# The two borders of a recurrent layer: squares of x while the context is read, sums by column tiles, factors spread ahead of the barrier, context added by GpSimd

## The reference

```python
for layer in range(2):
    shift_l, scale_l, gate_l = split(silu(c) @ ada_w[layer] + ada_b[layer])      # and shift_c, ... for the context
    hl = rmsnorm(xl, norm_pre[layer]) * (1.0 + scale_l) + shift_l
    hc = rmsnorm(xc, norm_pre[layer]) * (1.0 + scale_c) + shift_c
    oc, ol = even_mixer(hc, hl, ...) if layer == 0 else odd_mixer(hc, hl, ...)
    xl = xl + gate_l * rmsnorm(ol, norm_post[layer])
    if layer == 0:
        xc = xc + gate_c * rmsnorm(oc, norm_post[layer])
```

## Time and profile before

| | us |
|---|---|
| three executions | 3513.63, 3516.14, 3526.28 |
| the profiled execution | 3518.56 |
| its span in the profile | 3516.8 |
| PE busy | 3212.9 (91%), 18471 instructions |
| DVE busy | 1626.2 (46%) |
| POOL busy | 1342.6 (38%) |
| ACT busy | 1194.6 (34%) |

### The profile page before, as it was taken

The page is one execution under the profiler, slowest core; times in us unless marked ns, Lnnn a source line. Parts: engine busy times, 40 slices in busy tenths (PEclk is TensorE's granted clock), DMA queues, the critical chain, the costliest instruction groups (busy, mean ns, idle before and its releaser), DMA issues. The chain is left out here.

```text
span 3516.8 us, 49237 instructions
## 1 busy us (share of the span) xinstructions
PE 3212.9 (91%) x18471; PEld 2593.2 (74%) x18471; DVE 1626.2 (46%) x3082; ACT 1194.6 (34%) x2125; POOL 1342.6 (38%) x877
## 2 busy tenths in 40 slices
PE   6999988899998999898999959985988999989996
PEld 5888765688877888676788848873766777768875
DVE  6444386444435653412711044326666645264443
ACT  3222245322223222343322232243444434243342
POOL 3444431344443443333344423242666630133332
PEclk8999989899998999899999979996999999979998
DMA  7555321355544545222433332222222233112211
GB/s 228 187 178 173 112 76 35 120 185 181 171 132 156 175 135 159 76 78 66 141 95 92 98 113 60 70 80 61 49 51 45 62 85 106 36 48 60 60 49 42
DMA packets 636826, 363.03 MB, mean 103 GB/s; under 512 B 109182, under 2 KB 629108, under 8 KB 636144
## 3 DMA queue, kind: packets, MB, share of 16 engines
q1 hardware_dynamic: 632432, 353.48, 34.2%
q10 hardware_dynamic: 3056, 6.29, 0.5%
q0 software_dynamic: 1168, 0.91, 0.1%
HBM read 334.12 MB, written 26.50 MB: 103 GB/s over the span
## 5 line engine op out<-in xcount | busy, mean ns | idle before, releaser
L266 POOL TENSOR_TENSOR w_lo<-w_raw,w_hi 128x1024 fp32r<-128x1024 f32 (+1 forms) x398 | 939.8, 2362 | 1735.7 <-ACT w_hi L258 1735.7
L303 PE MATMUL acc<-h,w_hi 128*128 128x512 f32 x3136 | 978.7, 393 | 6.4 <-POOL w_lo L266 6.4
L258 ACT ACTIVATE w_hi<-w_raw 128x1024 fp32r<-128x1024 f32 (+1 forms) x398 | 414.4, 1042 | 996.5 <-PE acc L303 960.9
L303 PEld LDWEIGHTS acc<-h,w_hi 128*128 128x128 f32 x3136 | 584.0, 188 | 128.5 <-POOL w_lo L266 7.5
L303 PE MATMUL acc<-h,w_lo 128*128 128x512 f32 x1568 | 613.4, 391 | 0.0
L303 PE MATMUL acc<-hid,w_hi 128*128 128x512 f32 x1408 | 437.2, 392 | 0.0
L303 PE MATMUL lat<-h,w_hi 128*128 128x512 f32 x912 | 336.6, 407 | 16.0 <-DVE h L428 13.8
L303 PEld LDWEIGHTS acc<-h,w_lo 128*128 128x128 f32 x1568 | 295.0, 188 | 63.7
L707 DVE SCALAR_TENSOR_TENSOR ada_part<-ada_raw,c_act,ada_part 128x256 f32<-128x256 f32 x672 | 314.9, 488 | 18.6
L303 PEld LDWEIGHTS acc<-hid,w_hi 128*128 128x128 f32 x1408 | 263.6, 188 | 54.3
L303 PE MATMUL acc<-hid,w_lo 128*128 128x512 f32 x704 | 275.1, 391 | 0.0
(11 more groups left out here) (495 smaller groups left out, 5001.3 us busy)
## 6 DMA issues: line engine op xcount, KB each, us to landing
w_raw<-in_ffn_w SPq DMA_DIRECT2D x240, 512.0 KB, 3.9
ada_raw<-in_ada_w SPq DMA_DIRECT2D x88, 1024.0 KB, 5.0
w_raw<-in_od_w_in SPq DMA_DIRECT2D x32, 512.0 KB, 4.0
w_raw<-in_ev_w_in SPq DMA_DIRECT2D x30, 512.0 KB, 3.8
w_raw<-in_ffn_w SPq DMA_DIRECT2D x32, 384.0 KB, 3.4
image<-inverse_wait SPq DMA_DIRECT2D x288, 32.0 KB, 2.1
first_ada<-in_ada_w SPq DMA_DIRECT2D x8, 1024.0 KB, 12.3
w_raw<-in_ab_w_in SPq DMA_DIRECT2D x16, 512.0 KB, 3.9
```

The lines of the kernel that those rows point to most:

```text
L258: act.activation(K.w_hi[:, first % SPLIT, 0:tiles, :], K.raw[:, first % RAW, 0:tiles, :], ACT.Copy).then_inc(K.hi_ready, 1)
L266: pool.tensor_tensor(K.w_lo[:, first % SPLIT, 0:tiles, :], K.raw[:, first % RAW, 0:tiles, :], K.w_hi[:, first % SPLIT, 0:tiles, :].bitcast ...
L303: mm = pe.matmul(out, w[:, slot, k, :], moving(ap, k, tokens), start=first and k == 0 and p == 0, stop=last and k == tiles - 1 and p == le ...
```

## The change

In `even_in_phase` the norm is split in two. ACT squares x alone at once, PE sums the squares of each block directly with `sums_pe` (no adding by DVE), accumulating in a PSUM bank, and the roots and their inverse are made 128 columns wide; the context is transposed in between, and its squares, sums, roots and spread follow, in two tiles of 128 tokens. The splits of the first two weight chunks stand between the steps on ACT. The DVE coefficients (`mu`) come first instead of after the copies.

At the end of `even_out_phase` new functions with `wide_` names take the place of `norm_pe`, `post_dve`, `post_pool` and the `carry_` functions: three column tiles of 256 tokens instead of one-column products, the last block squared before it is copied and summed by PE on its own, the context of all blocks added by POOL, even blocks of x by POOL and odd ones by DVE through PSUM, and the factors for the next layer spread by PE ahead of the barrier into two PSUM banks, `K.spread`, that outlive it. `odd_phase` no longer spreads or waits for a spread.

```diff
@@ norm_dve
-    dve.wait_ge(N.spread, 1)
+    if carried != "spread":
+        dve.wait_ge(N.spread, 1)
@@ new functions
+THIRD = TOK // 3
+def wide_sums_pe(pe, K, out, src, start, stop):
+    for c in range(3):
+        mm = pe.matmul(out[32 * c:32 * c + 32, 0:THIRD], K.ones[:, 0:32], src[:, c * THIRD:(c + 1) * THIRD],
+                       start=start, stop=stop)
+    return mm
+def wide_spread_pe(pe, K):
+    for c in range(3):
+        mm = pe.matmul(K.spread[c // 2][:, (c % 2) * THIRD:(c % 2 + 1) * THIRD],
+                       K.ident[0:96, 32 * c:32 * c + 1].broadcast_to([96, P]), K.roots[0:96, :], start=True, stop=True)
+    return mm
+def wide_roots_act(act, K, sums):
+    return act.activation(K.roots[0:96, :], sums[0:96, 0:THIRD], ACT.Sqrt, scale=1.0 / D, bias=K.eps[0:96])
+def wide_post_pe(pe, K, S, sums):
+    pe.wait_ge(S.post.ssq_added, DB - 1)
+    wide_sums_pe(pe, K, sums, K.ssq, True, False)
+    pe.wait_ge(S.post.sq_ready, DB)
+    wide_sums_pe(pe, K, sums, K.sq[:, (DB - 1) % 2], False, True).then_inc(S.post.ssq_done, 1)
+    pe.wait_ge(S.post.rstd_ready, 1)
+    wide_spread_pe(pe, K).then_inc(S.post.spread, 1)
+def wide_post_dve(dve, K, S, gates, gain, banks):
...
+    for b in range(DB):
+        own, slot = b % 2, (b // 2) % 2
+        if b >= 4:
+            dve.wait_ge((S.x_even, S.x_odd)[own], b // 2 - 1)
+            if own:
+                dve.wait_ge(S.c_odd, b // 2 - 1)
+        lat = banks[slot][:] if own else K.sq[:, slot, LAT]
+        con = (K.ssq, K.var)[slot][:, 0:CTX] if own else K.sq[:, slot, CON]
+        dve.scalar_tensor_tensor(lat, S.y[:, b, LAT], K.fac[:, 0, b:b + 1], K.spread[0][:], ALU.mult, ALU.mult)
+        dve.scalar_tensor_tensor(con, S.y[:, b, CON], K.fac[:, 1, b:b + 1], K.spread[1][:, 0:CTX], ALU.mult,
+                                 ALU.mult).then_inc(S.scaled, 1)
+        if own:
+            dve.wait_ge(S.scaled, b + 1)
+            dve.tensor_tensor(K.x[:, b, :], K.x[:, b, :], lat, ALU.add).then_inc(S.x_odd, 1)
+def wide_post_pool(pool, K, S):
+    for b in range(DB):
+        slot = (b // 2) % 2
+        pool.wait_ge(S.scaled, b + 1)
+        if b % 2:
+            pool.tensor_tensor(K.xc[:, b, :], K.xc[:, b, :], (K.ssq, K.var)[slot][:, 0:CTX], ALU.add).then_inc(S.c_odd, 1)
+        else:
+            pool.tensor_tensor(K.x[:, b, :], K.x[:, b, :], K.sq[:, slot, LAT], ALU.add)
+            pool.tensor_tensor(K.xc[:, b, :], K.xc[:, b, :], K.sq[:, slot, CON], ALU.add).then_inc(S.x_even, 1)
+def wide_carry_pe(pe, K, S, sums):
+    for b in range(DB):
+        pe.wait_ge(S.carry.sq, b + 1)
+        mm = wide_sums_pe(pe, K, sums, S.y[:, b], b == 0, b == DB - 1)
+    mm.then_inc(S.carry.sum, 1)
+    pe.wait_ge(S.carry.root, 1)
+    wide_spread_pe(pe, K)
...
@@ even_in_phase, scalar
-                for n in range(SPLIT):
-                    split_hi(act, K, seg, n, n, 0, DB)
-                act.wait_ge(S.copied, DB)
-                pre_act(act, K, S, pre_mods)
+                act.activation(K.rstd[:, 0:1], K.eps, ACT.Sqrt)
+                for b in range(DB):
+                    if b >= 2:
+                        act.wait_ge(S.x_summed, b - 1)
+                    act.activation(K.sq[:, b % 2, LAT], K.x[:, b, :], ACT.Square).then_inc(S.x_squared, 1)
+                split_hi(act, K, seg, 0, 0, 0, DB)
+                act.wait_ge(S.x_summed, DB)
+                act.activation(root_x, con[0][:, 0:P], ACT.Sqrt, scale=1.0 / D, bias=K.eps).then_inc(S.x_root, 1)
+                split_hi(act, K, seg, 1, 1, 0, DB)
+                for b in range(DB):
+                    act.wait_ge(S.copied, b + 1)
+                    if b >= 2:
+                        act.wait_ge(S.c_summed, b - 1)
+                    act.activation(K.sq[:, b % 2, CON], K.xc[:, b, :], ACT.Square).then_inc(S.c_squared, 1)
+                act.wait_ge(S.c_summed, DB)
+                act.activation(root_c, con[1][0:64, 0:P], ACT.Sqrt, scale=1.0 / D, bias=K.eps[0:64]).then_inc(S.c_root, 1)
+                pre_act(act, K, S, pre_mods, "spread")
@@ even_in_phase, vector
+                dve.wait_ge(S.x_root, 1)
+                dve.reciprocal(root_x, root_x).then_inc(S.x_inv, 1)
+                for b in range(DB):
+                    dve.wait_ge(S.turned, b + 1)
+                    dve.tensor_copy(K.xc[:, b, :], lat[b % 4][:, 0:CTX]).then_inc(S.copied, 1)
+                dve.wait_ge(S.c_root, 1)
+                dve.reciprocal(root_c, root_c).then_inc(S.c_inv, 1)
@@ odd_phase
-        R = [S.psum(f"ret{i}", [P, 512]) for i in range(3)]
+        R = [*K.spread, S.psum("ret2", [P, 512])]
-                norm_pe(pe, S.pre, K, R[0:2], TOK, True)
@@ second_block, ahead of even_out_phase
+        K.spread = [K.psum(ctx, f"factors{i}", [P, 512]) for i in range(2)]
```

More of the change, by code:

```diff
@@ new lines, in wide_post_pool, with wide_carry_act @@
+def wide_post_pool(pool, K, S):
[7 more added lines that the diff above has]
+            pool.tensor_tensor(K.xc[:, b, :], K.xc[:, b, :], K.sq[:, slot, CON], ALU.add).then_inc(S.x_even, 1)
+def wide_carry_act(act, K, S, sums):
+    for b in range(DB):
+        act.wait_ge((S.x_even, S.x_odd)[b % 2], b // 2 + 1)
+        if b % 2:
+            act.wait_ge(S.c_odd, b // 2 + 1)
+        act.activation(S.y[:, b, LAT], K.x[:, b, :], ACT.Square)
+        act.activation(S.y[:, b, CON], K.xc[:, b, :], ACT.Square).then_inc(S.carry.sq, 1)
+    act.wait_ge(S.carry.sum, 1)
+    wide_roots_act(act, K, sums).then_inc(S.carry.std, 1)
@@ L2773, in even_out_phase @@
         unread = S.sb("unread", [P, 1])
+        K.roots = S.sb("norm_roots", [P, THIRD])
         mo = S.sb("m", [P, 2, DB, TOK], F32R)
         S.y = u
-        bank = [S.psum(f"out{i}", [P, 512]) for i in range(8)]
+        bank = [S.psum(f"out{i}", [P, 512]) for i in range(6)] + K.spread
         zc = u[:, ZC_ROW:ZC_ROW + 4, :].rearrange("p b t -> p (b t)")
```

87 lines of the change are left out of this document (68 added, 19 removed).

## The result

| | before | after |
|---|---|---|
| median, us | 3514.89 (6 executions, 3509.61 to 3526.28) | 3498.48 (6 executions, 3493.02 to 3502.54) |
| ratio to before | | 0.9942, 95% interval 0.9929 to 0.9956 |
| profiled execution, us | 3518.56, span 3516.8 | 3498.8, span 3497.0 |
| PE clock over the span | 0.944 | 0.946 |

The forecast was 3497.9 us, a range of 3491 to 3503, and more likely than not a gain beyond 0.5%. The ratio means 20.4 us less (15.5 to 25), the two medians alone 16.4, and the sum of the three terms was 18.2. The interval's slow end, 0.9956, does not reach the forecast's 0.5%, so the gain is certain, but not that it passes 0.5%.

A forecast was written before the change was run, and what follows sets the result against it. At the two borders engines wait for each other in one chain, so time cut there comes off the whole. 10.3 + 7.6 + 0.3 = 18.2 us, from 3516.14 to 3497.9 us; 8-in-10 range 3491 to 3503.

The forecast's parts named there:

- First border, forecast 10.3: First border: DVE's first scaling comes at 2078.1, with half clock up to 2071.6 and full clock in the loop; gain 10.3 us.
- The context loop: First border: eight visits of context sums and four transposed blocks; 6.4 us at half clock, about 3.9 at full, 3.9 taken.
- the chain through two buffers: First border's context loop: sum frees buffer, ACT squares, PE sums; 0.8 us for two blocks, later than PE's 3.2.
- The tail: First border, behind the context loop: root, inverse, spread of four records and handovers; 2.2 to 2.8 us, 2.6 taken.
- Second border up to the phase's start, forecast 7.6: Second border: last output product to next phase's start; that phase starts at 3094.8 instead of 3102.42, gain 7.6 us.
- Behind the barrier, forecast 0.3: Odd phase's start: spread gone but DVE's h lo waits for POOL's w_lo; PE starts at 6.7 against 6.92, gain 0.3 us.
- PE was not at half clock throughout: Rival at both borders: PE stays at half clock; with late POOL, total gain 12.6 to 15.5 us; joint chance 0.27.
- POOL was not late: Same rival, second border's scaling: POOL's slower context additions take up to 2.9 us off the gain; joint chance 0.27.
- DVE did not pass POOL: Rival behind the barrier: both h lo precede POOL's second w_lo, PE starts 2.3 us sooner; more-than-forecast chance 0.22.
- the dense stretch kept 1.00: Rival: dense stretches lose the full clock; 36 us more of half clock eats the whole gain; chance 0.03.
- the context landed 6.6 us after the start: Rival at first border: context lands later, each microsecond costing one, 3500.9 at 3 us late; chance 0.04.
- the 24 that the forecast had named as a sign of being wrong: Whole kernel: a gain outside 12.6 to 24 us, or anywhere but in the two stretches, would be wrong.

The follow-up runs named there:

- four-buffer run: Changed kernel with four buffers instead of two for the squares at the first border; first border 16.26 us against 16.76, a single execution.
- The pieces: Changed kernel with POOL making the odd phase's second w_lo in four pieces, each behind one block's h; second border 32.50 us, ratio 0.992 to the kernel before.
- x in SBUF: Changed kernel with the odd blocks' scaled x in SBUF instead of a PSUM bank; second border 34.83 us, ratio 0.9935 to the kernel before.
- after, again: Changed kernel, unedited, timed again on another chip; median 3493.84 us against 3523.44 for the kernel before, ratio 0.9915.
- the four runs on the first of the three chips: Against the kernel before: first border's change alone 0.9941, second's alone 0.9965; changed kernel with spread behind the barrier 0.9904, with second w_lo in pieces 0.992.
- best: Changed kernel with spread behind the barrier, second w_lo in pieces and four tiles of 192 columns; second border 30.26 us, ratio 0.991 to the kernel before.
- before, again: Kernel before, unedited, profiled a second time as a single execution; 867.46 us to the even output phase, span 3515.6 us.
- one more root: Kernel before plus one 128x1 root on ACT at the start of the input phase; ratio 0.9995, 869.88 us to the even output phase.
- the run with the second border alone: Kernel before with only the second border's part of the change; second border 34.58 us, median 3512.05 us, ratio 0.9965.
- the one with a longer first border: Kernel before plus 14 chained ACT squares at the first border; first border 36.54 us, ratio 1.0039.
- the spread behind the barrier: Changed kernel with the odd layer's spread put back behind the barrier; second border 31.84 us instead of 34.57, ratio 0.9904 to the kernel before.
- the two best versions: The changed kernel with spread behind the barrier, w_lo pieces and four 192-column tiles, without and with four first-border buffers; ratios 0.991 and 0.9922 to the kernel before.

## Why the prediction was right

- **First border, forecast 10.3, measured 10.35.** The start is as worked out: x sums done before the context lands, transposes at +6.6, half clock there, and the full clock behind the spread (1.00 in 2078 to 2081). Three sizes were off, and it is luck that they cancelled to within 0.1 us. The context loop was put at 3.9 and took 4.56: the forecast had named the chain through two buffers as the bound at the full clock and counted PE at 3.2 for eight visits. In the first four visits PE itself is the bound, at 0.71 a visit; the four-buffer run shows it, and that each change between 32-column sums and transposes costs 0.20 us from start to start, where the forecast priced the two kinds as if they stood alone. The tail was put at 2.6 and took 2.29, and the loop began 9.9 us after the memset where 10.3 was forecast.
- **Second border up to the phase's start, forecast 7.6, measured 7.6.** The odd phase starts 27.9 us after ACT's first instruction behind the last product (3055.57 to 3083.45), for 35.5. The inverse of 1.75 (1.74), the spread of 2.93 (2.9), the pair of 2.82 (2.83), POOL's 1.27 and 0.73 (1.27 and 0.7), all from rows of other shapes, scaled by columns. The three-tile sums run about 1.0 a block at half clock.
- **Behind the barrier, forecast 0.3, measured 0.2.** PE's wait was forecast as 6.7 and is 6.69, by the mechanism named: DVE's h lo (two SBUF inputs) held by POOL's two w_lo, each getting its turn: forecast ends of 4.1, 6.25 and 6.5 us for h lo, the second w_lo and h lo again, measured 4.1, 6.27 and 6.55. The pieces show it by taking POOL away. By the Trainium skill (SBUF — State Buffer, "Who interferes with whom") such a pair excludes each other for whole instructions, and an instruction of DVE with at most one SBUF input, outside its 2-port modes, stays out of it. The trace agrees: two blocks take 2.82 us where DVE's addition has one SBUF input (the changed kernel), and 3.06 where it has two (x in SBUF).
- **What the forecast did not see** is that this term hid a loss, so the part that it booked as a gain was right in size and wrong as advice. It compared the wait behind the barrier with the one before (6.7 and 6.92) and booked the difference; but the spread's 2.9 us ahead of the barrier were inside the term of 7.6. Read as one part, "spread ahead of the barrier" moves 2.93 us from a place where ACT and POOL covered them to one where nobody does, and costs 2.7.
- **The rivals.** PE was not at half clock throughout (the loop ran at 1.00) and POOL was not late (the price of up to 2.9 us for that was too high: with the 1.57 and twice the 0.90 of the earlier trace rows two blocks take 3.37 us instead of 2.83, 2.2 for all eight); DVE did not pass POOL; the dense stretch kept 1.00; the context landed 6.6 us after the start, for 6.5. Of the slower side nothing came.
- **The whole time is partly luck.** In the first timing the changed kernel took 3498.48 us, for 3497.9, and the stretches outside the borders gave little. In the second timing (*after, again*) its 3493.84 us lie in the forecast's range, but the gain, 24.7 to 35.2 us by its interval, lies beyond the 24 that the forecast had named as a sign of being wrong, and the part above 18.4 comes from stretches that it said would give nothing. What it got right are the borders.
- **The rest of the difference stays open.** Four executions of kernels in which no border is shorter took 863.4 to 869.9 us to the even output phase (mean 866.8), ten with a shorter one 857.7 to 864.4 (mean 860.6), though no instruction is edited there. The times say the same: of nine timings of kernels with a shorter border, six (the four runs on the first of the three chips, *after, again* and *best*) have an interval wholly above what their borders gave. By the middle of the ratios the surplus is 4 to 13 us, and 2 in the first timing. So scatter alone is an unlikely account of it. The way from the first scaling to the first preparation of the scan is 231.3 to 232.5 or 235.2 to 236.2 us, in kernels of either kind, so most of the difference does not lie there. The scan behind it, to the start of its last state product, takes 621.8 to 630.4 us in the edited kernels and 624.8 to 635.8 in the others. The granted clock has a part in that: in the changed kernel the scan took 621.9 us at 0.92 and, again, 630.4 at 0.90. It is not all. The scan in the profile after, and in that of *before, again*:

```profile
2319.00:2940.88 621.88, 543.00 (x5480) 423.58 (x5478) 372.48 (x830) 269.01 (x755) 322.25 (x387) 0.92 0.24 58
```

```profile
2324.64:2953.54 628.90, 545.47 (x5479) 427.28 (x5478) 376.26 (x830) 269.16 (x755) 320.65 (x387) 0.92 0.24 59
```

At the same clock and with 2.5 us more of PE busy the second is 7.0 longer. It is not a shift of the instructions like that of one more root (635.8), and not the length of the first border (the run with the second border alone has 860.41 to the even output phase, the one with a longer first border 863.41). No run tells what does it.

## What to carry to other kernels

Cut the trace into stretches at events that both kernels have, and read an edit of 10 us from its stretch: the borders here repeated to 0.5 us, while a stretch that nobody edited took from 858 to 870. Before you move work ahead of a barrier, ask what covers it where it is now: a 2.9 us spread beside weight splits was free, and cost 2.7 when it was moved away from them. Where two engines hold each other up, as DVE's h lo and POOL's w_lo do here, give the one on the path its turn first (smaller pieces behind a semaphore), or keep one of its operands in PSUM.

## What the runs showed of the hardware

The clock that PE finds when it comes back from a wait is not the same in each execution. After 9 us of dense products at 1.00 and a few short sums, PE waits 2.36 us for the same inverse. The same six records of the first spread then took 2.93 us in both profiles of the changed kernel and in those with the second border alone, the spread behind the barrier and the pieces, 2.53 in the four-buffer run, and 1.97 in the run with x in SBUF. From the profile after and from the last:

```profile
3046.00:3055.00 9.00, 9.00 (x53) 7.88 (x53) 0.96 (x1) 1.64 (x4) 0.00 (x0) 1.00 0.00 0
3059.50:3062.40 2.90, 2.90 (x6) 1.84 (x6) 0.00 (x0) 0.00 (x0) 0.00 (x0) 0.50 0.00 0
```

```profile
3041.00:3050.00 9.00, 9.00 (x53) 7.89 (x52) 0.96 (x1) 1.64 (x4) 0.00 (x0) 1.00 0.00 0
3054.30:3056.30 2.00, 1.97 (x6) 1.15 (x6) 0.00 (x0) 0.00 (x0) 0.00 (x0) 0.76 0.00 0
```

The granted clock is 0.50 in the one and 0.76 in the other, with the same work ahead of it: it fell to half as the spread began in the one, and 1.0 us later in the other. So a border's time has a term of up to 1 us that moves without an edit, and the second border of the run with x in SBUF has to be read without it. With the first spread put at its half-clock length in each (2.93 us, or 3.11 for ten records), the borders agree: 34.57 us for both the changed kernel and the four-buffer run, 30.68 for the two best versions, and 35.79 with x in SBUF, 1.2 more than the changed kernel.
